# Attention in a hybrid decoder block: which engine copies a unit's first and which its second transpose round out of PSUM

## The reference, cut to what matters

```
s_s = jnp.einsum('bqhgd,bhqsd->bhgqs', qc, ks).astype(f32) * scale + bias_s
p_s = _masked_softmax(s_s, (dist_s >= 0)[:, :, None])
o_s = jnp.einsum('bhgqs,bhqsd->bqhgd', p_s.astype(dtype), vs)
...
s_w = jnp.einsum('bqhgd,bkhd->bhgqk', qc, kw).astype(f32) * scale + bias_w
p_w = _masked_softmax(s_w, valid_w)
o_w = jnp.einsum('bhgqk,bkhd->bqhgd', p_w.astype(dtype), vw)
...
o = g[..., 0:1] * o_cmp + g[..., 1:2] * unblock(o_sel) + g[..., 2:3] * unblock(o_win)
```

## Time and profile before

| | us |
|---|---|
| runs | 1022.12, 1019.69, 1024.54 |
| median | 1022.12 |
| profiled execution | 1021.36 |
| its span (first to last instruction) | 1019.5 |
| attention stage in it | 357.3 to 549.7 |

### The profile page before, as it was taken

How to read it: one execution, slowest core, us unless ns; L and a number is a source line. 1 busy time by engine, 2 the same in 40 slices (tenths; PEclk the granted TensorE clock), 3 DMA queues, 4 the chain that set the end, 5 groups by cost and what they waited for, 6 DMA issues and landing times. The chain is left out here.

```text
span 1019.5 us, 14663 instructions
## 1 busy us (share of the span) xinstructions
PE 957.4 (94%) x5691; PEld 567.2 (56%) x5691; DVE 493.3 (48%) x1259; ACT 278.2 (27%) x658; POOL 139.3 (14%) x136
## 2 busy tenths in 40 slices
PE   6999999999899989999999999996999997999993
PEld 4534787766465466677775555563544443444441
DVE  2487393079635467777773224275631111211126
ACT  3210110120322367787863101120000000100023
POOL 3000000032201011111101000011022221212220
PEclk9999999999999989999999999986999998999997
DMA  9310231050600092000000324657789999999976
GB/s 264 119 45 4 83 59 25 0 48 9 179 2 0 1 274 66 2 2 2 2 2 2 143 105 165 260 196 267 293 286 364 395 397 394 391 391 395 394 217 266
DMA packets 67127, 165.89 MB, mean 163 GB/s; under 512 B 38219, under 2 KB 40299, under 8 KB 54695
## 3 DMA queue, kind: packets, MB, share of 16 engines
q1 hardware_dynamic: 58928, 146.16, 40.0%
q0 software_dynamic: 7840, 18.25, 7.1%
q10 hardware_dynamic: 288, 0.53, 0.2%
HBM read 147.41 MB, written 25.24 MB: 169 GB/s over the span
## 5 line engine op out<-in xcount | busy, mean ns | idle before, releaser
L2071 PE MATMUL banks<-shared,wout 128*128 128x512 f32 (+1 forms) x384 | 137.8, 610 | 7.8 <-issue 6.1
L1667 PE MATMUL banks<-wout,shared 128*128 128x512 f32 x256 | 112.7, 594 | 0.5 <-PEq L1303 0.5
L1370 ACT ACTIVATE shared<-shared,low 128x640 f32<-128x640 f32 (+7 forms) x128 | 93.7, 736 | 9.1 <-DVE low L1458 8.7
L2071 PEld LDWEIGHTS banks<-shared,wout 128*128 128x128 f32 (+1 forms) x384 | 53.3, 170 | 75.8 <-issue 75.3
L386 PE MATMUL banks<-x,wout 128*128 128x512 f32 x192 | 86.4, 606 | 0.8 <-DVE x L427 0.8
L2134 DVE SCALAR_TENSOR_TENSOR mix_bt<-mix_bt,slot_coef,banks 128x256 f32<-128x256 f32 x24 | 11.5, 480 | 149.0 <-ACT mix_bt L2114 148.9
L1401 PE MATMUL banks<-shared 64*128 64x512 f32 (+3 forms) x384 | 77.0, 485 | 4.6 <-DVE low L1458 3.2
L1667 PEld LDWEIGHTS banks<-wout,shared 128*128 128x128 f32 x256 | 47.6, 190 | 55.2 <-issue 55.2
L1439 PE MATMUL banks<-shared 128*64 128x128 f32 x1056 | 69.2, 279 | 1.3 <-DVE mix_tmp L1522 1.3
L1422 PEld LDWEIGHTS banks<-consts,shared 64*128 64x128 f32 x1056 | 48.2, 140 | 30.6 <-issue 9.5
L2024 POOL DMA_INDIRECT x_rows<-wout,tok x22 | 35.5, 1614 | 207.0 <-DVE wout L2141 161.9
(11 more groups left out here) (364 smaller groups left out, 1314.5 us busy)
## 6 DMA issues: line engine op xcount, KB each, us to landing
shared<-in_exp_w_down SPq DMA_DIRECT2D x24, 1024.0 KB, 25.5
shared<-in_exp_w_gate SPq DMA_DIRECT2D x24, 1024.0 KB, 20.4
shared<-in_exp_w_up SPq DMA_DIRECT2D x24, 1024.0 KB, 26.7
x<-in_exp_w_down SPq DMA_DIRECT2D x8, 1024.0 KB, 29.2
wout<-in_w_in SPq DMA_DIRECT2D x16, 256.0 KB, 5.1
wout<-in_w_in SPq DMA_DIRECT2D x2, 2048.0 KB, 8.7
x<-in_x SPq DMA_DIRECT2D x1, 4096.0 KB, 28.4
x_rows<-x SPq DMA_DIRECT2D x8, 512.0 KB, 2.6
```

What stands on the lines that cost most here:

```text
L1370: nc.scalar.activation(prob[:, u % 2, at:at + n], prob[:, u % 2, at:at + n], ACT.Exp, bias=low[:, u % 2, v, j:j + 1], scale=-1.0, accum_ou ...
L1667: ins = nc.tensor.matmul(psum[n % 4], src[:, i * P:i * P + P], m["wout"][:, k, half * 512:half * 512 + 512], start=k == 0, stop=k == KD - 1)
L2071: ins = nc.tensor.matmul(psum[2 + p][rows].rearrange("p (a f) -> p a f", a=2), xt[:, p, k, rows], wgu[b][:, :, k], start=k == 0, stop=k == ...
```

## The change

In tiles 2 to 7 the two engines change places: the first round is taken by DVE and the second by ACT. The exceptions are now two: a first round that ends in mixing weights is taken by both (three units: the first of tile 2, the first of tile 4, and the first window unit of tile 7), and a second round that ends in mixing weights, or has a further round behind it, is taken by both as before. Tiles 0 and 1 and PE's queue don't change.

```
-        at_dve = [ON_DVE] if c == 0 else [BOTH] if c == 1 else [ON_ACT, BOTH if here[1][-1][0] == "w" or late else ON_DVE]
+        at_dve = [ON_DVE] if c == 0 else [BOTH] if c == 1 else [ON_DVE if here[0][-1][0] == "p" else BOTH, BOTH if here[1][-1][0] == "w" or late else ON_ACT]
```

## The result

The changed kernel takes **1041.08 us** (1038.55 to 1042.94, 3 runs) against 1022.12: ratio 1.0195, 95% interval 1.017 to 1.022. So it is slower beyond the noise; whether by more than 2% the interval leaves open. The forecast was 1041.5. The profiled execution took 1041.08 with a span of 1039.2, so against that of before 19.7 us, and the stage alone explains it. It ran from 355.2 (first scores) to 567.5 (first matmul of the output projection), 212.3 us; before from 357.3 to 549.7, 192.4.

A forecast was written before the change was run, and what follows sets the result against it. The attention stage's ring of engine queues bounds the kernel, PE first, with DVE's loop just under it. Terms of +15.6 and +3.8 give +19.4 on 1021.4, so 1040.8, adjusted to 1041.5; range 1029 to 1055.

The forecast's parts named there:

- The loop: DVE's cycle in the attention stage: score pass, first round's copies, second score pass, next scores; 3.73 against 3.20 at 640 keys.
- 2P + E + 0.08 + R: Shortest turn: P one score pass, E the pair of copies, 0.08 read-out, R restart until the next first pass.
- The slack: Before the change, DVE's loop of 2.8 lay under PE's turn of 3.20 at 640 keys, leaving 0.4.
- The 31 turns: Attention-stage turns from the first round at 422.09 to that at 541.69; 119.60 us before, forecast +15.6.
- Coefficients: At branch ends DVE's mix coefficients wait for ACT's last exponential, now behind second-round copies; 6.0 over the 31 turns.
- loop and mixes: The 31 turns without coefficients: 128.6 for the loop against 119.6 before, plus 0.6 where mixes delay the first score pass.
- Tiles 2 and 3 and the end: Longer four-pass turns in tiles 2 and 3, coefficients entering tile 3, and the last unit; together +3.8.
- r1 to ACT: Second round's copies moved to ACT stay hidden under the next unit's scores; gain nothing beyond a few tenths.
- The cover holds: Rival: outputs and the 0.4 us of slack absorb the copies; stage stays at 192, time 1022; chance 0.08.
- Faster: Rival: taking first-round copies off ACT shortens PE's weight-load waits by up to 10.4, giving 1012; chance 0.04.
- The clock falls: Rival: new PE gaps halve the granted clock at eight changes of branch, up to 3 us each, 1066; chance 0.06.
- The signs named: What the profile after should show in the attention stage: 210 to 213 long instead of 192, turns near 504 of 3.7.

The follow-up runs named there:

- coef_after_b1: Changed kernel with the coefficients computed behind DVE's second score pass instead of ahead of the first: 1030.35 us, ratio 1.0105.
- before_coef: Kernel before the change with the coefficients computed behind DVE's second score pass instead of ahead of the first: 1017.86 us, ratio 0.9984.
- only_r0: Half of the change on the kernel before: first round's copies go to DVE, second round's stay on DVE: 1037.55 us, ratio 1.0165.
- only_r1: Other half of the change on the kernel before: second round's copies go to ACT, first round's stay on ACT: 1023.37 us, ratio 1.0016.
- r1_act_coef: Kernel before with the second round's copies on ACT and coefficients behind DVE's second score pass: 1016.80 us, ratio 0.9958.
- half_coef: Changed kernel with each first round split between DVE and ACT and coefficients behind DVE's second score pass: 1023.41 us, ratio 1.0021.
- r0_both: Changed kernel with every first round from tile 2 on split, one copy each for DVE and ACT: 1029.11 us, ratio 1.0088.
- dummy_mid: Kernel before plus two unused additions per unit on DVE between its two score passes, from tile 2 on: 1048.77 us, ratio 1.0271.
- evict_last: Changed kernel with the first round's copies behind DVE's second score pass instead of between the passes: 1073.66 us, ratio 1.0517.
- the two dummy kernels: dummy_mid, and the kernel before with such additions behind DVE's second score pass instead: 1032.39 us, ratio 1.0115.

## Why the prediction was right

- **The loop.** 2P + E + 0.08 + R gave 3.73 at 640 keys and 5.17 at 1024; measured 3.70 and 5.12. At 640 two errors cancel. The parts are 0.75 (b0), 0.80 (copies; I had 0.89, not less their overlap with b1), 0.82 (b1 with its read-out) and 1.33 (from the read-out to b0; I had 1.28, counted from PE's first load and so 0.05 short), together 3.70. From 517.79 to 521.55 it is 3.76, because a mix holds b0 up by about 0.05. The 5.12 is one turn; the two others of that length took 4.99 and 4.81, and those of 768 and 896 keys 4.09 to 4.15 and 4.39 to 4.63, where 4.2 and 4.7 were forecast.
- **The slack.** "Its slack of 0.4 is what the kernel lives on" was mis-sized. It was taken as PE's 3.20 less DVE's 2.8, but a read-out of b1 costs as soon as it comes behind PE's first load of the scores, and that left 0.12 at this place. For a pair of copies it made no odds, since R came from the earlier trace rows, where PE had stalled. For half a pair it did: 3.45 and 3.52 where the sum has 3.3.
- **The 31 turns.** r0 starts at 424.10 and 558.85 in the trace after, 134.75 us apart against 135.2 forecast and 119.60 before: +15.15 against +15.6.
- **Coefficients** (6.0 in these turns, 1.27 at the entry to tile 3). Turn by turn, what the changed kernel has over coef_after_b1, less what the kernel before has over before_coef, is 1.8 at the entry to tile 4 (forecast 1.8), 0.66 behind the 1024-key units (1.0), 0.0 to 0.66 at the six others (0.4 to 0.75), together 4.5, and 0.95 at the entry to tile 3. So this term was 1.8 too large with both (7.3 in the forecast, 5.45); loop and mixes, 9.6 in the forecast, took 15.15 - 4.5 = 10.6, one too small. The forecast laid the coefficients wholly on ACT's copies. only_r0 shows that these make 3.9 us of the changed kernel's excess; the rest is that coefficients stand in a loop that has no slack left.
- **Tiles 2 and 3 and the end.** The turns of tiles 2 and 3 became 3.4 longer as forecast (with the unit whose round is split 0.46 shorter, forecast 0.3), the last two 0.4. Another 0.5 lies in the first tiles, which the change doesn't touch, and where kernels with the same code differ as much. That the total is only 0.4 off is therefore partly luck: a coefficient term 1.8 too large stands against 1.0 too little for the loop and 0.5 that no term had.
- **r1 to ACT**, "nothing beyond a few tenths": in the profiled executions it gains 0.8 us of stage where the coefficients don't stand in the loop (190.1 to 189.3), which the runs can't tell from nothing, and loses 2.7 where they do, with r0 still on ACT. The forecast had that loss, but under the coefficients.
- **The rivals.** "The cover holds" fell: even one copy costs 4.7 us. It was also what the rule of the Trainium skill, Perfetto Trace Analysis, section Optimizing Scalar/DVE Operations, would give if one takes an engine that isn't saturated as free; here one at 75% was not, and busy time sorts the kernels wrongly (DVE is equally idle in only_r1 and r1_act_coef, 6 us apart; half_coef and r0_both have DVE as before and are slower). The 2.9 us more engine time that the prediction estimated from that section's figures compare with 2.3 measured (DVE and ACT together, 289.2 before and 291.5 after). "Faster" has its grain: with r1 off DVE and the coefficients moved there are 4 us to win, but by keeping r0 on ACT. "The clock falls" didn't happen in tiles 2 to 7 of the changed kernel, where PE stood at most 1.74 us at once; in dummy_mid it fell behind a gap of 2.58, in evict_last behind 3.06.
- **The signs named.** Stage 210 to 213 (212.3), copies x110 and x66, DVE's idle before L1359 nearly gone (3.0) and before L1458 over 20 (27.6), PE and its loads waiting for DVE: 16.4 + 7.2 + 9.6 + 3.1 = 36 us. All came. For L1458's low it was not "in nearly every unit", though: 19 loads and 7 matmuls are listed in 40 units, and in others, as at 519.91, the stall is drawn as longer matmuls.

## What to carry to other kernels

Before moving an instruction to the engine that seems free, write down the loop of queues that passes through the place where it will stand, with the restart of the one who waits; if the loop is within the instruction's length of the longest one, the move costs the difference in every turn, whatever the engine's share of busy time. The same work behind the last instruction of the loop cost less than half, and taking a small waiting step (coefficients) out of it gained. When slack is read off a timeline, its end is where the waiting engine begins to load, and not the difference of two loops. And before a restart is called longer than another, look at what else stands ahead of the restarted instruction in its own queue, and count both from the same event.

## What I had not expected of the hardware

DVE's additions between two SBUF operands took 0.48 to 1.77 us each in dummy_mid, at widths of 320 to 512; without POOL beside them 0.48 to 0.69. Of its timeline, at two places (POOL's row at the first):

```profile
519.39 1.28 POOL L1541 TENSOR_TENSOR shared<-shared,mix_tmp 128x512 f32<-128x512 f32 x1 [3.40 <-DVE mix_tmp L1530]
...
519.97 1.45 DVE L1488 TENSOR_TENSOR spent<-consts 128x320 f32<-128x320 f32 x2
```

```profile
496.41 0.89 DVE L1488 TENSOR_TENSOR spent<-consts 128x320 f32<-128x320 f32 x2
```

The same pair took 0.89 where POOL was idle and 1.45 where POOL's addition was running until 520.67. The Trainium skill, SBUF — State Buffer, section Who interferes with whom, says that a DVE instruction with two SBUF inputs contends with a GpSimd instruction that reads SBUF; the trace agrees. The pair of copies out of PSUM shown above took 0.88 and 0.89. So additions in SBUF stand in well for copies from PSUM as long as POOL does nothing, and poorly beside its additions; the stages of the two dummy kernels hold both, which is why they were read turn by turn above.
